# A two-block transformer kernel: modulation's bias added by VectorE, a split output product, another front and two filler steps a round

## What is computed

```
mod = silu(c) @ ada_w + ada_b          # six rows of 1024: shift1, scale1, gate1, shift2, scale2, gate2
h   = rms_norm(x) * (1 + scale1) + shift1
x   = x + gate1 * token_mixer(h)       # in-projection; attention and two gated linear scans;
                                       # merged = g0*(att @ w_a) + g1*(hg @ w_b); merged @ w_out
h   = rms_norm(x) * (1 + scale2) + shift2
x   = x + gate2 * experts(h)           # router picks 64 tokens for each of 16 experts;
                                       # 24 MB of weights for each expert
```

## Time and profile before

| what | value |
|---|---|
| median of 3 runs | 2147.46 us (2144.62 to 2148.29) |
| the profiled execution | 2146.76 us, its span 2145.0 us |
| PE, DVE, ACT busy | 1955.7, 655.5, 431.4 us (91, 31, 20% of the span) |
| mean granted clock | 0.968 |
| DMA | 513.44 MB, 239 GB/s over the span |

### The profile page before, as it was taken

The page is one execution under the profiler, slowest core; times in us unless marked ns, Lnnn a source line. Parts: engine busy times, 40 slices in busy tenths (PEclk is TensorE's granted clock), DMA queues, the critical chain, the costliest instruction groups (busy, mean ns, idle before and its releaser), DMA issues.

```text
span 2145.0 us, 20603 instructions
## 1 busy us (share of the span) xinstructions
PE 1955.7 (91%) x8842; PEld 1181.7 (55%) x8842; DVE 655.5 (31%) x923; ACT 431.4 (20%) x657; POOL 27.8 (1%) x41
## 2 busy tenths in 40 slices
PE   5999889999969999888988999888899999999998
PEld 4876766567733434343433434343344488888887
DVE  6375464562230020101102020111028713222333
ACT  4357444310110101010000101010020313222222
POOL 0000000000000000000000000000030000000000
PEclk9999989998979999999999999999989999999999
DMA  7211201576419999999999999999962023333210
GB/s 291 84 54 49 70 21 40 205 266 227 165 66 418 417 417 417 416 416 416 418 418 418 417 417 416 416 417 417 396 203 79 20 62 115 98 98 98 99 59 40
DMA packets 151232, 513.44 MB, mean 239 GB/s; under 512 B 8035, under 2 KB 78819, under 8 KB 116195
## 3 DMA queue, kind: packets, MB, share of 16 engines
q1 hardware_dynamic: 146768, 487.95, 58.2%
q10 hardware_dynamic: 4374, 24.18, 3.0%
HBM read 510.00 MB, written 2.10 MB: 239 GB/s over the span
## 4 chain that ended last, share of the span: by engine, by line
PE 67%; DMA 21%; DVE 7%; ACT 3%; issue 2%; SPq 0%; POOL 0%; ACTq 0%; DVEq 0%; POOLq 0%
DMA work<-in_w_exp_up 11%; PE ps L1077 10%; DMA ring<-in_w_exp_up 7%; PE ps L510 6%; PE ps L533 5%; PE ps L1231 5%; PE ps L1038 5%; PE ps L1190 4%; PE ps L1192 4%; PE ps L1191 4%; PE ps L965 3%; PE ps L526 3%; PE ps L528 3%; PE ps L527 3%; PE ps L696 1%
## 5 line engine op out<-in xcount | busy, mean ns | idle before, releaser
L1038 PE MATMUL ps<-work 128*64 128x512 f32 x1208 | 358.0, 595 | 34.1 <-DMA work<-in_w_exp_up 33.3
L1038 PE MATMUL ps<-ring,work 128*64 128x512 f32 x720 | 220.5, 595 | 19.6 <-DMA ring<-in_w_exp_up 19.1
L1038 PEld LDWEIGHTS ps<-work 128*64 128x64 f32 x1208 | 116.5, 137 | 210.7 <-issue 147.0
L2071 DVE TENSOR_TENSOR work<-work,ps 64x512 f32<-64x512 f32 x64 | 42.0, 692 | 498.2 <-ACT work L1564 497.5
L1564 ACT ACTIVATE work<-ps 64x512 f32<-64x512 f32 x64 | 32.6, 584 | 751.2 <-PE ps L1038 751.2
L510 PE MATMUL ps<-work,ring 128*128 128x512 f32 x320 | 139.2, 593 | 1.2 <-ACT work L1461 0.8
L1038 PEld LDWEIGHTS ps<-ring,work 128*64 128x64 f32 x720 | 72.2, 137 | 123.1 <-issue 83.6
L1077 PE MATMUL ps<-work 128*64 128x512 f32 x560 | 135.4, 630 | 4.2 <-issue 3.6
L1190 PE MATMUL ps<-xh,wh 128*128 128x512 f32 x352 | 137.0, 389 | 0.0
L1192 PE MATMUL ps<-xh,wl 128*128 128x512 f32 x352 | 136.9, 389 | 0.0
L1191 PE MATMUL ps<-xl,wh 128*128 128x512 f32 x352 | 136.9, 389 | 0.0
(11 more groups left out here) (276 smaller groups left out, 2461.4 us busy)
## 6 DMA issues: line engine op xcount, KB each, us to landing
work<-in_w_exp_gate SPq DMA_DIRECT2D x76, 1024.0 KB, 24.5
work<-in_w_exp_up SPq DMA_DIRECT2D x75, 1024.0 KB, 26.4
work<-in_w_exp_down SPq DMA_DIRECT2D x70, 1024.0 KB, 21.0
ring<-in_w_exp_gate SPq DMA_DIRECT2D x45, 1024.0 KB, 24.2
ring<-in_w_exp_up SPq DMA_DIRECT2D x45, 1024.0 KB, 25.9
ring<-in_w_exp_down SPq DMA_DIRECT2D x42, 1024.0 KB, 22.1
ring<-in_w_in SPq DMA_DIRECT2D x27, 1024.0 KB, 5.5
work<-in_ada_w ACTq DMA_DIRECT2D x16, 1024.0 KB, 5.5
```

Of the source, the lines that this page charges most:

```text
L1038: i = e.matmul(PS[64 * gu:64 * gu + 64, fb, :], at(XET + 128 * k + 64 * z, 64), flat(key)[:, 512 * fb:512 * fb + 512], start=(k == 0), sto ...
```

## The change

- The biases of modulation's second and third parts are added by VectorE: after the last piece of each it adds the one row `ADAB` to partition 0 of the sum. `ada_cols` and `ada_row` lose their bias products.
- `w_out` is read as four pieces of 512 by 512. ScalarE and VectorE make upper and lower parts of them and of `MG` (`wo_hi`, `wo_lo`, `merged_hi`, `merged_lo`), and TensorE makes 192 products of 512 columns instead of 128 float32 products of 256. Its units are now a half of the columns by one row block, so a row block can be normed after each of units 4 to 7. `w_out`'s first piece is loaded earlier.
- Front: TensorE takes `ada` piece 0 instead of 3; ScalarE scales the rows of x; the rows are turned as they come, six tiles of them ahead of the shift; scale is finished before shift; shift comes in two halves; the first two units of the in-projection go side by side.
- The weave has two filler steps a round, not three.
- The cycle of slots and the waits of their first pieces are others. `eps6` and `eps5` move from one constant table to another.

```diff
-    slots = [1, 2, 3, 0, 4, 5, 1, 2] + [3 + i % 3 for i in range(len(keys) - 8)]
+    slots = [2, 1, 3, 0, 4, 5, 1, 0] + [3 + i % 3 for i in range(len(keys) - 8)]
...
+    i = more.index(("c0", 3))
+    keys += more[:i] + [("wo", 0)] + more[i:] + [("wo", i) for i in range(1, 4)]
+    slots.insert(len(slots) - len(more) + i, 16)
+    slots += [4, 5, 0]
...
-    cycle = (8, 16, 12, 13, 14, 9, 1, 2, 10, 15, 7, 11, 3, 4, 5, 0, 6)
+    cycle = (12, 13, 14, 15, 8, 16, 2, 4, 7, 11, 9, 10, 1, 5, 3, 0, 6)
...
+        MGL = part("mgl", MG, 4096)
+        WOH = [part("woh0", SLOT[8], 2048)[:, :], FWH[0][:, :], FH[:, 2048:4096], FWL[3][:, :]]
+        WOL = [part("wol0", SLOT[16], 2048)[:, :], FWL[4][:, :], FWL[5][:, :], FH[:, 0:2048]]
...
+                r0, c0 = 512 * (key[1] % 2), 512 * (key[1] // 2)
+                return t["w_out"][r0:r0 + 512, c0:c0 + 512].rearrange("(k p) n -> p k n", p=128)
...
+                if key == ("wo", 0):
+                    e.wait_ge(s["mg_m"], 1)
...
+                    if slot in (8, 2):
+                        e.wait_ge(s["wo_pe"], 4)
+                    elif slot in (9, 10, 1, 3):
+                        e.wait_ge(s["wo_pe"], 8)
                     elif slot in (12, 13, 14):
                         e.wait_ge(s["mg_pb"], 8)
                         e.wait_ge(s["mg_m"], 4)
-                    elif slot == 9:
-                        e.wait_ge(s["mg_m"], 8)
-                    elif slot in (10, 15):
+                    elif slot == 15:
                         e.wait_ge(s["mg_m"], 8)
                         e.wait_ge(s["d_ada"], 24)
                     elif slot in (7, 11):
-                        e.wait_ge(s["ac_pe"], 3)
+                        e.wait_ge(s["ac_pe"], 5)
...
-            def ada_cols(acc, half, bk, o, bias):
+            def ada_cols(acc, half, bk, o):
                 for i in range(8):
-                    n = half * 1024 + 128 * i
-                    p = e.matmul(bank(bk, 1, o + i), at(acc + n, 128), ones[:, 0:1], start=True, stop=not bias)
-                    if bias:
-                        p = e.matmul(bank(bk, 1, o + i), rows(0, 1, ADAB + n, 128), rows(0, 1, O_CST + CST["ones"][0], 1),
-                                     start=False, stop=True)
+                    p = e.matmul(bank(bk, 1, o + i), at(acc + half * 1024 + 128 * i, 128), ones[:, 0:1], start=True, stop=True)
...
+            e.wait_ge(s["d_small"], 1)
+            e.wait_ge(*got["ada", 0])
             for i in range(8):
                 for b in range(2):
-                    e.matmul(bank(7, 1, 8 + i), piece(("ada", 3), 2)[:, b, 128 * i:128 * i + 128], at(cact + 6 + b, 1), start=(i + b == 0), stop=False)
-            e.wait_ge(s["d_ada"], 3)
+                    e.matmul(bank(7, 1, 8 + i), piece(("ada", 0), 2)[:, b, 128 * i:128 * i + 128], at(cact + b, 1), start=(i + b == 0), stop=False)
+            e.wait_ge(s["d_ada"], 4)
             for i in range(8):
-                e.matmul(bank(7, 1, 8 + i), at(ACC + 1024 + 128 * i, 128), ones[:, 0:1], start=False, stop=(i == 7))
-            def turn_1(k):
+                p = e.matmul(bank(7, 1, 8 + i), at(ACC + 1024 + 128 * i, 128), ones[:, 0:1], start=False, stop=(i == 7))
+            p.then_inc(s["ac_pe"], 1)
+            def turn_1(k, c):
+                return e.transpose(bank(k, 128, 128 * c), at(XS + 1024 * c + 128 * k, 128), ident)
+            for c in range(TC):
+                e.wait_ge(*normed(1, c))
+                for k in range(6):
+                    i = turn_1(k, c)
+                    if c == TC - 1:
+                        i.then_inc(s["t_pe"], 1)
...
+                        if (pr, g) == (0, 0):
+                            hT_ready(0)
+                            dense_w(0, key, 0, [0])
+                            for k in range(1, 8):
+                                hT_ready(k)
+                                p = dense_w(0, key, 0, [k])
+                                dense_w(1, key, 1, [k - 1])
+                            p.then_inc(s["hp_pe"], 1)
+                            dense_w(1, key, 1, [7]).then_inc(s["hp_pe"], 1)
+                        elif (pr, g) != (0, 1):
+                            dense_w(bk, key, g % 2).then_inc(s["hp_pe"], 1)
...
-            weave(lv, fill, att, fill, att, fill)
+            weave(lv, fill, att, fill, att)
             def ada_row(acc, n, bk):
-                e.matmul(bank(bk), ones, at(acc + n, 512), start=True, stop=False)
-                e.matmul(bank(bk), one_row, rows(0, 1, ADAB + n, 512), start=False, stop=True).then_inc(s["ar_pe"], 1)
+                e.matmul(bank(bk), ones, at(acc + n, 512), start=True, stop=True).then_inc(s["ar_pe"], 1)
...
+            for a in range(2):
+                for tc in range(TC):
+                    u = 4 * a + tc
+                    wo_free(u)
+                    for k in range(KD):
+                        q = 2 * a + k // 4
+                        if tc == 0 and k % 4 == 0:
+                            e.wait_ge(s["fs_l"], q + 1)
+                        if u == 0:
+                            e.wait_ge(s["sx_l"], k + 1)
+                        o, w = 512 * k + 128 * tc, slice(512 * (k % 4), 512 * (k % 4) + 512)
+                        e.matmul(bank(u % 6), FL[:, o:o + 128], WOH[q][:, w], start=(k == 0), stop=False)
+                        e.matmul(bank(u % 6), FL[:, o:o + 128], WOL[q][:, w], start=False, stop=False)
+                        p = e.matmul(bank(u % 6), MGL[:, o:o + 128], WOH[q][:, w], start=False, stop=(k == KD - 1))
+                    p.then_inc(s["wo_pe"], 1)
+                    second_gate(u)
...
+            e.wait_ge(s["d_small"], 2)
+            for c in range(TC):
+                e.activation(at(XS + 1024 * c, 1024), at(X0 + 1024 * c, 1024), ACT.Identity, scale=at(st1 + 4 + c, 1)).then_inc(s["r_d"], 1)
...
-                    e.wait_ge(s["d_ada"], 8)
+                    e.wait_ge(s["t_pe"], 1)
...
-                if k == 0:
-                    e.wait_ge(s["sc1"], 1)
+                if k in (0, 4):
+                    e.wait_ge(s["sc1"], 2 + k // 4)
...
+            def wo_hi(i):
+                e.wait_ge(*got["wo", i])
+                if i == 0:
+                    e.wait_ge(s["ac_pe"], 4)
+                    e.wait_ge(s["ar_pe"], 2)
+                elif i < 3:
+                    e.wait_ge(s["mg_gb"], 4)
+                else:
+                    e.wait_ge(s["mg_pb"], 8)
+                e.activation(WOH[i], flat(("wo", i)), ACT.Copy).then_inc(s["fs_h"], 1)
+            def merged_hi(k):
+                e.wait_ge(s["mg_m"], k + 1)
+                if k == 0:
+                    e.wait_ge(s["mg_gb"], 4)
+                e.activation(FL[:, 512 * k:512 * k + 512], at(MG + 512 * k, 512), ACT.Copy).then_inc(s["sx_h"], 1)
...
+                if d == 7:
+                    wo_hi(0)
...
+            merged_hi(0)
+            merged_hi(1)
+            wo_hi(1)
+            for k in range(2, 8):
+                merged_hi(k)
+            wo_hi(2)
+            wo_hi(3)
...
+                if k == 7:
+                    own(m)
+                    e.wait_ge(s["l_ab"], 16 * (i // 8) + 16)
+                    m = e.tensor_tensor(rows(0, 1, acc, 2048), rows(0, 1, acc, 2048), rows(0, 1, ADAB, 2048), ALU.add)
...
-            for k in range(3):
+            for k in range(1, 5):
...
-            rms(1, X0, XS, st1, range(4), lambda c: None)
+            e.wait_ge(*rooted(1, 3))
+            e.reciprocal(at(st1 + 4, 4), at(st1 + 4, 4)).then_inc(s["d_small"], 1)
             for k in range(5, 8):
                 ada_step(k, ACC)
+                if k == 5:
+                    e.wait_ge(s["ac_pe"], 1)
+                    e.scalar_tensor_tensor(out=at(sc1, 8), in0=bank(7, 8, 8), scalar=1.0, in1=vec("nmw"), op0=ALU.add, op1=ALU.mult).then_inc(s["sc1"], 1)
...
+            def shift_half(i):
+                e.wait_ge(s["ac_pe"], 2 + i)
+                e.tensor_copy(at(sh1 + 4 * i, 4), bank(7 - i, 4, 4 * i)).then_inc(s["sc1"], 1)
+                e.wait_ge(s["sc1"], 2 + i)
+            shift_half(0)
...
+                if k == 0:
+                    shift_half(1)
+                elif k == 1:
+                    half_lo(1)
...
+            def wo_lo(i):
+                e.wait_ge(s["fs_h"], i + 1)
+                e.tensor_tensor(WOL[i], flat(("wo", i)), WOH[i].bitcast(F32), ALU.subtract).then_inc(s["fs_l"], 1)
+            def merged_lo(*ks):
+                for k in ks:
+                    x = slice(512 * k, 512 * k + 512)
+                    e.wait_ge(s["sx_h"], k + 1)
+                    e.tensor_tensor(MGL[:, x], at(MG + 512 * k, 512), FL[:, x].bitcast(F32), ALU.subtract).then_inc(s["sx_l"], 1)
...
+                    if d == 7:
+                        wo_lo(0)
+                        merged_lo(0, 1)
...
+                if d == 7:
+                    merged_lo(2, 3)
+                    wo_lo(1)
...
+            merged_lo(4, 5, 6, 7)
+            wo_lo(2)
+            wo_lo(3)
```

(11 more changed lines are left out.)

180 lines of the change are left out of this document (71 added, 109 removed).

## The result

The changed kernel takes **2109.31 us** (median of 4 runs, 2108.04 to 2111.76) against 2147.03 for the kernel before in the same comparison: ratio 0.983, 95% interval 0.9815 to 0.984. The forecast was 2109.5. The profiled execution took 2108.66, with a span of 2106.9.

A forecast was written before the change was run, and what follows sets the result against it. The experts' weight stream was taken to bound the kernel through its start; gains of 2.9 + 3.6 + 5.5 + 24.2 + 1.3 = 37.5 us put the first expert product at 594.7 and the time at 2109.5, range 2103 to 2123.

The forecast's parts named there:

- What bounds: Experts' weight stream: its end follows its start, so each us the first expert product comes earlier is a kernel us.
- Front: Start of the kernel: first split product at 41.0, 2.3 earlier; gain 2.9 us in all, bounds 1 to 4.
- The half us for the units side by side: In the front: running the in-projection's two first units side by side saves half a us between them.
- Weave: Scan and attention rounds with two filler steps: fewer waits, gain 3.6 us, bounds a loss of 5 to a gain of 6.
- Merge: Stretch before the output product: bias products gone and clock perhaps kept, 5.5 us earlier, bounds 3 to 7.
- The 0.5 charged for VectorE's additions and `w_out`: In the merge: 0.5 us lost to VectorE's two row additions with work queued behind, and `w_out`'s first piece competing for DMA.
- Output product: Split products of 0.227 us and sums without bias end it at 558.4; 24.2 us gained, bounds 18 to 25.5.
- Norm, router: Behind the output product: one row block left to norm instead of two, 1.3 us less, bounds 0 to 2.
- Fillers missed: Rival in the weave: TensorE waits longer for shares and keys, loss of 5 for gain of 3.6; 2118, chance 0.14.
- The split in the path: Rival at the output product: making upper and lower parts delays the first unit by ten us; about 2124, chance 0.08.
- Lower clock: Rival: whole split output product at the lower clock, 43.6 us more; 2153, slower by 5.6, chance 0.03.
- The change that doesn't reach the end: Rival: pieces are missing when the experts begin, 15 of 17 needed, and the stream ends as before; chance 0.03.

The follow-up runs named there:

- the kernel with the block: Changed kernel with modulation's bias again as TensorE products, the output stage's one-column products in a row behind a unit; 2126.83 us (0.9913).

## Why the prediction was right, point by point

- **What bounds.** Right, and shown from two sides: one for one over 60 us of first expert product (from 572.31 up, with 1511.8 to 1513.2 behind it in all kernels but the one that holds pieces back), and 25.6 us lost where the pieces were held back.
- **The sum** is closer than its terms. The weave came 1.3 and the merge 0.7 short of the forecast, the output product 0.7 and norm and router 1.0 above it, and the front is known to 2 us only. That 37.4 stands beside 37.5 is in part luck.
- **Front.** 3.1 for 2.9. VectorE's end at 34.9 was measured at 34.8, the last turns at 38.94 for 38.8 (the sum's own terms, 34.9 + 1.0 + 2.6, give 38.5), the first product at 40.56 for 41.0. The half us for the units side by side was not there; the eight turns took 1.6 instead of 2.2 up to the first product.
- **Weave.** The term was mis-sized: 2.3 for 3.6. I had taken the wait of 2.67 on the keys' copy as gone with the third filler step. It was replaced by four of 0.66, 1.28, 0.66 and 1.39, 4.0 together, since ScalarE still has attention's copy ahead of the keys'. TensorE's waits in the weave fell from 11.1 to 9.2 only. With keys first on ScalarE the weave is 2.7 shorter still.
- **Merge.** 4.8 for 5.5, by two errors that nearly cancel. The bias was worth 7.4, of which I had 5.0 for the work and 1.0 for the clock. The 0.5 charged for VectorE's additions and `w_out` should have been 2.6 (to the end of its last record the merge with the bias on TensorE takes 114.2, before 111.6), and for another cause: with the bias back on TensorE the wait is 2.74, so it isn't the additions. It is the meeting of SP's piece ("c0", 2) with ScalarE's loads. The meeting that I had named and taken as nearly free was another, that of `w_out`'s first piece, which is issued at 421.77 only; the one that cost I had not seen. The Trainium skill's rule that I had set against the term, "DMA: Bandwidth & Descriptors", section on queues, rings and completion order, fits this other pair: by it I had put 2.5 us at most, and the first `ada_w` piece was taken up 2.5 us later after its issue where SP's piece was under way.
- **Two fillers as a whole** were thus worth nothing by the stages (2.3 - 2.9, and 2.2 - 2.4 in the kernel before) and at most 1.6 us by the medians, not 3.6: the step that failed is that a stage's gain was summed without asking which load its new end would meet.
- **Output product.** 24.9 for 24.2, in its parts too: 47.6 us for the 48.4 of the sum. The product of 0.227 carried over to other tiles, 10.7 of gain, and VectorE's parts, done by 509, kept nobody. I had named the columns' clock as a part of the gain, 6 us if it came again; it is 5.1 in the kernel with the block and 6.9 in the kernel before.
- **Norm, router.** 2.3 for 1.3. Up to the nine turns of the last row block the stretch fell from 5.54 (588.04 - 582.50) to 4.17 (551.53 - 547.36), 1.4 for the 1.3 of the step. Behind it another 0.9 went, which I had not counted. It is no more than the scatter of this stage among kernels that are equal there, 46.9 to 48.2.
- **Rivals.** Fillers missed: not at two, fully at one. The split in the path: not at three products, 2.00 of it at one. Lower clock: it did not come; every ten from 500 to 550 is at 1.00, though the output product cycles through six banks. So what the Trainium skill says in "TensorE: Matmul & The Clock Gate", section on a second failure mode, is not seen here. The change that doesn't reach the end: not even with SP's queue held back by 85 us, when 11 us of the gain were left.

## What to carry to other kernels

Find the one event from which all behind it is fixed, show it one for one, and sum the stages before it. For each stage that ends earlier or later, list which transfers of other queues are now issued at that moment: a gain of 2.3 us went back this way, and an earlier load in a free slot recovered 1.9. A block of one-column products can cost more than its duration, since the clock falls for the products behind it; a sum that another engine can do on one line, beside full products, removes both. And compare stages between the same kind of borders: an end of a record here and a start there moved 0.6 us from one stage to the next.

## What the runs showed of the hardware

- An addition of 1x2048 on VectorE takes 2.28 us, the subtraction of 128x2048 that makes a lower part 2.28 to 2.29: one partition is as long as 128.
- With a block of 32 records of one-column products the granted clock was 0.57 in the ten from 520 to 530, and a pair went from 0.38 to 0.58 us inside the block; with blocks of 16 records (1.84 us), and with the same columns between full products, it stayed at 1.00.
- Behind a wait of 2.47 us ahead of split products the clock was 0.73 in the next window of five us (430 to 435); behind waits of 0.64 and 1.02 it stayed at 1.00.
- In the stream a piece of 1.048 MB takes 2.51 us. One issued on SP's queue together with three loads of ScalarE's queue was taken up 8.6 us after its issue, and the first `ada_w` piece of the other queue 12.1 to 12.3 us after its own, 2.5 more than the 9.5 to 9.7 without it.
